# Token-major projections: four PSUM banks in turn instead of twelve matmuls to one

## The reference, cut to what matters

```python
proj = h @ w_in[l]                                    # first block: q, k, v, o, gates, z, u, qc
kv = mn @ w_kv                                        # memory keys and values (km, vm)
x = x + jnp.concatenate([y_a, y_b, y_c], axis=-1) @ w_out[l]
p = jnp.einsum('btd,de->bte', h, w_in[l]) + b_in[l]   # second block: a_u, a_v, q, k, v, r, ...
h = layer_norm(DEEPNORM_ALPHA * h + m @ w_out[l], ln1_g[l], ln1_b[l])
f = jnp.square(jax.nn.relu(h @ w_ff1[l])) @ w_ff2[l]
h = layer_norm(DEEPNORM_ALPHA * h + f, ln2_g[l], ln2_b[l])
```

## Time and profile before

| | |
|---|---|
| executions | 1139.32, 1141.18, 1141.46 us; median 1141.18 |
| span of the profiled execution | 1139.6 us (the profile gives no other time for it) |
| PE busy | 1114.3 us, 98% of the span, 5404 matmuls |
| PEld busy | 934.6 us, 82% |
| DVE, ACT, POOL busy | 601.2, 419.0, 85.9 us |
| mean DMA rate | 101 GB/s |
| mean granted TensorE clock | 0.989 |

### The profile page before, as it was taken

How to read it: one execution, slowest core, us unless ns; L and a number is a source line. 1 busy time by engine, 2 the same in 40 slices (tenths; PEclk the granted TensorE clock), 3 DMA queues, 4 the chain that set the end, 5 groups by cost and what they waited for, 6 DMA issues and landing times.

```text
span 1139.6 us, 13000 instructions
## 1 busy us (share of the span) xinstructions
PE 1114.3 (98%) x5404; PEld 934.6 (82%) x5404; DVE 601.2 (53%) x668; ACT 419.0 (37%) x446; POOL 85.9 (8%) x95
## 2 busy tenths in 40 slices
PE   8999999999999999999699999999999999999996
PEld 8788888887888888888588888888888888888885
DVE  5553357546544565558465654766332334435446
ACT  7444442543343422343333633332232223332330
POOL 3000000000022000006200000121000000000002
PEclk8999999999999999999799999999999999999999
DMA  8523421223324422231222222361423323323221
GB/s 280 180 77 111 147 75 40 82 74 111 111 75 159 126 104 74 80 124 38 74 74 74 77 72 74 108 224 59 126 78 106 109 75 111 98 86 111 78 70 74
DMA packets 82737, 114.79 MB, mean 101 GB/s; under 512 B 4316, under 2 KB 57948, under 8 KB 82560
## 3 DMA queue, kind: packets, MB, share of 16 engines
q1 hardware_dynamic: 79648, 103.19, 27.7%
q0 software_dynamic: 2752, 10.76, 2.7%
q10 hardware_dynamic: 288, 0.13, 0.0%
HBM read 109.87 MB, written 4.20 MB: 100 GB/s over the span
## 4 chain that ended last, share of the span: by engine, by line
PE 89%; DVE 5%; POOL 2%; issue 2%; ACT 1%; DMA 0%; DVEq 0%; POOLq 0%; SPq 0%; ACTq 0%
PE bank L369 27%; PE bank L371 27%; PE bank L370 27%; PE bank L477 2%; PE bank L671 1%; DVE w_lo L1162 1%; POOL rstd_tmp L1781 1%; DVE residual L1599 1%; PE bank L597 1%; PE bank L578 1%; DVE bn L1466 1%; PE bank L727 1%; PE bank L630 1%; PE bank L615 1%; DVE v_hat L1473 1%
## 5 line engine op out<-in xcount | busy, mean ns | idle before, releaser
L1162 DVE TENSOR_TENSOR w_lo<-w_raw,w_hi 128x2048 fp32r<-128x2048 f32 (+1 forms) x92 | 209.7, 2281 | 281.3 <-ACT w_hi L871 279.1
L369 PE MATMUL bank<-act_t_hi,w_hi 128*128 128x512 f32 (+1 forms) x832 | 321.4, 386 | 11.2 <-ACT u_gelu L1048 10.7
L371 PE MATMUL bank<-act_t_hi,w_lo 128*128 128x512 f32 (+1 forms) x832 | 318.2, 382 | 0.0
L370 PE MATMUL bank<-act_t_lo,w_hi 128*128 128x512 f32 (+1 forms) x832 | 317.9, 382 | 0.0
L871 ACT ACTIVATE w_hi<-w_raw 128x2048 fp32r<-128x2048 f32 (+1 forms) x91 | 172.0, 1892 | 204.1 <-PE bank L371 191.6
L369 PEld LDWEIGHTS bank<-act_t_hi,w_hi 128*128 128x128 f32 x832 | 157.2, 189 | 41.8 <-issue 11.7
L371 PEld LDWEIGHTS bank<-act_t_hi,w_lo 128*128 128x128 f32 x832 | 157.0, 189 | 30.5
L370 PEld LDWEIGHTS bank<-act_t_lo,w_hi 128*128 128x128 f32 x832 | 157.3, 189 | 29.9 <-issue 0.2
L369 PE MATMUL bank<-w_hi,x_hi 128*128 128x512 f32 x416 | 162.2, 390 | 0.0
L371 PE MATMUL bank<-w_hi,x_lo 128*128 128x512 f32 x416 | 161.9, 389 | 0.0
L370 PE MATMUL bank<-w_lo,x_hi 128*128 128x512 f32 x416 | 161.8, 389 | 0.0
(11 more groups left out here) (262 smaller groups left out, 1077.6 us busy)
## 6 DMA issues: line engine op xcount, KB each, us to landing
w_raw<-in_w_in SPq DMA_DIRECT2D x46, 1024.0 KB, 5.1
w_raw<-in_w_ff SPq DMA_DIRECT2D x32, 1024.0 KB, 5.2
w_raw<-in_w_out SPq DMA_DIRECT2D x10, 1024.0 KB, 5.2
w_raw<-in_w_mem_kv SPq DMA_DIRECT2D x3, 1024.0 KB, 6.6
residual<-in_x SPq DMA_DIRECT2D x4, 512.0 KB, 9.6
x_spill<-residual POOLq DMA_DIRECT2D x1, 2048.0 KB, 7.1
residual<-x_spill POOLq DMA_DIRECT2D x1, 2048.0 KB, 9.7
out<-residual SPq DMA_DIRECT2D x3, 512.0 KB, 2.6
```

The source lines that it names most:

```text
L369: pe.matmul(dst, lh, rh, start=start, stop=False)
L370: pe.matmul(dst, lh, rl, start=False, stop=False)
L371: return pe.matmul(dst, ll, rh, start=False, stop=stop)
L1162: return dve.tensor_tensor(dst, src, hi.bitcast(f32), ALU.subtract)
```

## The change

In every weight block of a token-major accumulation but the last, the loops are turned around. A new helper goes, for each kk, through the tiles with high times high, then through the tiles with high times low, then with low times high, so that successive matmuls go to banks 2, 3, 4, 5 in turn. The last block keeps the old order, and so does `tm_pair`. In the first block (g = 0) all banks are taken before the first matmul. The number of matmuls and their operands are the same.

```diff
+            def three_rotating(tiles, lh, ll, rh, rl, start):
+
+                for j in range(tiles):
+                    pe.matmul(bank[2 + j][:, :], lh[:, tile_of(j)], rh, start=start, stop=False)
+                for j in range(tiles):
+                    pe.matmul(bank[2 + j][:, :], lh[:, tile_of(j)], rl, start=False, stop=False)
+                for j in range(tiles):
+                    last = pe.matmul(bank[2 + j][:, :], ll[:, tile_of(j)], rh, start=False, stop=False)
+                return last
...
 (tm_block)
-                for j in range(tiles):
+                if g < groups - 1:
+                    if g == 0:
+                        for j in range(tiles):
+                            take(2 + j, ("tm", n, j))
+                    for kk in range(4):
+                        xh, xl = lhs(kk)
+                        last = three_rotating(tiles, xh, xl, wh[:, kk, :], wlo[:, kk, :], g == 0 and kk == 0)
+                        if between and kk == 1:
+                            between()
+                for j in range(tiles if g == groups - 1 else 0):
                     key = ("tm", n - g, j)
-                    if g == 0:
-                        take(2 + j, key)
                     for kk in range(4):
                         xh, xl = lhs(kk)
                         last = three(bank[2 + j][:, :], xh[:, tile_of(j)], xl[:, tile_of(j)], wh[:, kk, :], wlo[:, kk, :],
-                                     g == 0 and kk == 0, g == groups - 1 and kk == 3)
-                    if g == groups - 1:
-                        give(last, key)
+                                     False, kk == 3)
+                    give(last, key)
...
 (group, the matmuls of ff2)
+                    if g < 7:
+                        if g == 0:
+                            for j in range(TT):
+                                take(2 + j, ("tm", n0, j))
+                        for kk in range(4):
+                            h, l = lhs(kk)
+                            last = three_rotating(TT, h, l, wh[:, kk, :], wlo[:, kk, :], g == 0 and kk == 0)
+                        last.then_inc(w_used, 1)
+                        return
                     for j in range(TT):
-                        key = ("tm", n0, j)
-                        if g == 0:
-                            take(2 + j, key)
                         for kk in range(4):
                             h, l = lhs(kk)
                             last = three(bank[2 + j][:, :], h[:, tile_of(j)], l[:, tile_of(j)], wh[:, kk, :], wlo[:, kk, :],
-                                         g == 0 and kk == 0, g == 7 and kk == 3)
-                        if g == 7:
-                            give(last, key)
-                    if g < 7:
-                        last.then_inc(w_used, 1)
+                                         False, kk == 3)
+                        give(last, ("tm", n0, j))
```

## The result

The changed kernel takes 1144.40 us (median of nine runs, 1143.01 to 1145.77); the kernel before, run beside it, 1140.15 us (nine runs, 1138.92 to 1141.63). The ratio is 1.0036, 95% interval [1.0026, 1.0046]: 4.2 us slower. The forecast was 4.1 us slower, 1145.3 us; that figure started from 1141.18 us for the kernel before, the median of the first three of these nine runs.

A forecast was written before the change was run, and what follows sets the result against it. PE, busy 98% of the span, was taken as the bound: number of matmuls times distance between starts, plus gaps. Rotation 0 and waits 1.11 + 1.18 + 1.24 + 0.58 = 4.11 us on 1141.2 gave 1145.3 us, range 1142.3 to 1147.8.

The forecast's parts named there:

- The distance does not change: In the 1128 rotated matmuls the distance between starts stays 226.7 ns, so the rotation itself costs 0.
- the bound before: Limit drawn from rows on the rotation's effect: 13.3 ns a matmul, 15.0 us saved or lost over 1128 matmuls.
- The four waits: At four first blocks PE waits for all banks before the first matmul: 4.11 us in all.
- the slow restart: After a wait the second matmul follows after 0.32 us, not 0.227: 0.09 us more where the block did not already start so.
- second half of `ff2`: PE waits for DVE's reader of bank 5 where this half starts: 1.02 + 0.09 = 1.11 us.
- second columns of `w_out`: PE waits for bank 5's reader where these columns start: 1.09 + 0.09 = 1.18 us.
- `v2`: At its start PE waits for DVE's cumulative sums over the gate logits in banks 2 to 5: 1.24 us.
- `o`: Behind `v`, PE waits for ACT to free bank 5: 0.58 us, the slow second matmul being there already.
- Nothing takes it back: The 10.7 us wait moves along, as the ACT and DVE work behind it waited for the last bank of `a_v`.
- A quicker stream: Rival: each rotated matmul saves 13.3 ns paid for repeating a bank, 15.0 us won, 4.1 lost: 1130.3 us; chance 0.06.
- Hidden waits: Rival: the waits at the takes are there but mostly hidden: 1141.2 to 1143.3 us; chance 0.10.
- Lost clock: Rival: the four gaps or the rotation drop the granted clock to 1.2 GHz, 9.8 us more: 1155 us; chance 0.04.

The follow-up runs named there:

- The late reader: Changed kernel plus two DVE subtractions between the last matmul to bank 5 in the first half of `ff2` and that bank's reader: 1146.90 us, ratio 1.0055.
- the two rotation runs: Changed kernel with rotation only in blocks neither first nor last: ratio 1.0000; with first blocks rotated over banks 2 and 3, then 4 and 5: 0.9997.
- takes alone: Kernel before, old matmul order, but all banks taken before the first matmul of each accumulation's first block: 1144.61 us, ratio 1.0033.
- the two late readers: Two DVE subtractions added ahead of bank 5's reader in the first half of `ff2`: in the changed kernel ratio 1.0055, in the kernel before 1.0000.
- the first four experiments: takes alone 1.0033; changed kernel with rotation only in blocks neither first nor last, 1.0000; rotation by pairs 0.9997; lazy takes 1.0015; kernel before beside them 1140.53 us.
- rotation by pairs: Changed kernel, but first blocks rotate over banks 2 and 3, then 4 and 5, each pair taken when needed: 1140.29 us, ratio 0.9997.
- lazy takes: Changed kernel, but each bank is taken just ahead of its own first matmul: 1142.42 us, ratio 1.0015.
- other banks: Changed kernel, but the second half of `ff2` accumulates in banks 6, 7, 0 and 1: 1143.65 us, ratio 1.0024.
- the second changed profile: Profile of the changed kernel run again, unmodified, on the same chip as other banks: 1145.67 us, ratio 1.0044.

## Why the prediction was right

*The distance does not change.* Forecast 0 for 1128 matmuls; measured 226.68 ns in the half of `ff2` that is mostly rotated, against 226.66, and a ratio of 0.9997 for all of them rotated with the takes out of the way. The interval of that run allows 1.4 us saved to 0.7 us lost, 1.2 ns saved to 0.6 lost a matmul; the bound before was 13.3. The comparison of a stretch with 12 matmuls to a bank to one with 24 had said so in advance. The Trainium skill (TensorE: Matmul & The Clock Gate, section "Wait — 56ns, not 53.3ns?") has 215.7 ns from start to start of back-to-back matmuls of 512 columns at full clock; the trace has 226.7 in every order tried, so the repeated bank is not what makes up the difference.

*The four waits.* The mechanism was the forecast one, and no term is off by more than 0.02 us, so the sum owes nothing to errors that cancel. Each term against its measure, the wait and the slow restart together:

| place | forecast | measured | from |
|---|---|---|---|
| second half of `ff2` | 1.11 | 1.12 | 1046.31 - 1045.06 - 0.227, + 0.10 (1.17 for four instead of 1.07) |
| second columns of `w_out` | 1.18 | 1.19 | 315.69 - 314.36 - 0.227, + 0.09 |
| `v2` | 1.24 | 1.26 | 402.45 - 401.05 - 0.227, + 0.09 |
| `o` | 0.58 | 0.60 | 110.05 - 86.44 against 110.65 - 87.64 |
| sum | 4.11 | 4.17 | 4.22 by the stretch from `v` to the end |

*What the working had wrong.* Two things, and neither is a term of the sum. The waits of 10.7 and 1.0 us are not "nearly all" of PE's list before: it adds up to 16.3 us, and 4.0 of the rest are the waits for `mem`, `ones` and `mem_t_lo` in the first 90 us, a stretch that the four takes don't touch. And three waits of 1.0 to 1.2 us were to show in the list, which has 0.87, 0.94 and 1.01: the list counts from the end of the last matmul's row, 0.39 us after its start, and the sum from where the next matmul would have started, 0.227 us after it. The median itself came out 0.9 us under the forecast 1145.3, since the kernel before ran at 1140.15 us and not at 1141.18.

*Nothing takes it back.* The 10.7 us wait for `u_gelu` is 10.7 us in both profiles: what PE waits for there moved along with PE. The late reader shows the same for one longer wait: 2.27 us more wait, 2.25 us more in `ff2`.

*The rivals.* A quicker stream is excluded by the two rotation runs. Hidden waits are excluded by takes alone and by the two late readers. Lost clock did not come: the mean granted clock is 0.990 after and 0.989 before, and in both profiles it is 1.00 from `v` to 537 us, with three of the four waits, and from 563 us to the end of `ff2`, with the fourth. The Trainium skill (same page, section "A second HAM failure mode: psum-queue depth-cycling") ties going round the banks to small idle bits and a swinging clock. Here 1128 matmuls went round the banks (four, two in `vm`), at the old distance and with no clock lost, and the gaps that the takes made cost their own length and 0.1 us of restart. In this kernel, going round the banks did not by itself bring what that section describes.

## What to carry to other kernels

When matmuls in a stream stand at the same distance whether the bank changes or not, the order of banks is free, and only what it does to the moment at which each bank must be free counts. An accumulation that reuses the banks of the one before it needs time between the last matmul to a bank and the first new one. At `ff2` that is 1.25 us from start to start: 0.42 until the reader starts (0.39 of it the matmul's own row), 0.69 for the reader, 0.14 until PE goes on. Tile by tile that time is filled by the other tiles' matmuls; rotated over all the banks there are none to fill it. If a rotation is wanted for another reason, rotating over half of the banks in the first block or taking other banks removed the wait here.

## What the runs showed of the hardware that was not expected

Runs of one kernel spread by 2 to 3 us, and the spread goes with the clock. Of the 28 executions of the kernel before beside the first four experiments, the six at a mean granted clock of 0.992 took 1139.55 to 1139.76 us, the eleven at 0.989 took 1141.21 to 1141.87. The profiles show two places where it can arise. One is the first 30 us: with a granted clock of 0.87 to 0.90 over 12 to 30 us `v` starts at 87.64 to 87.82 us (seven profiles), with 1.00 at 85.96 to 86.44 (three). The other is the stretch behind the single long wait. After the 10.7 us wait the matmuls stand 0.427 us apart until the clock comes back. In the profile of before that is so for eleven distances, ten of them between the two rows; in rotation by pairs it is so for five, though the wait was the same:

```profile
553.10 0.77 PE L369 MATMUL bank<-act_t_hi,w_hi 128*128 128x512 f32 x1 [10.72 <-ACT u_gelu L1075]
...
555.37 0.63 PE L371 MATMUL bank<-act_t_hi,w_lo 128*128 128x512 f32 x1
555.79 0.46 PE L369 MATMUL bank<-act_t_hi,w_hi 128*128 128x512 f32 x1
556.09 0.39 PE L370 MATMUL bank<-act_t_lo,w_hi 128*128 128x512 f32 x1
```

Six distances fewer at 0.2 us each are 1.2 us, which is the -1.26 of that run in the table. Late reader in the changed kernel has five as well (5.28 + 1.2 = 6.5, expected 6.6), lazy takes nine (0.98 + 0.4 = 1.4, expected 1.5), takes alone, other banks and the first changed profile twelve, the second changed profile eleven. Up to `ff2` the late reader's program is the changed one, so five, eleven and twelve come from one and the same order of instructions. The span of one profile can thus be off by over 1 us here, while the same wait agrees within 0.02 us from one kernel's profile to the next (0.87 us at `ff2` in the changed kernel and in takes alone).

The other thing is that in the profiled executions waits of PE of up to 3.1 us cost no clock, while the one of 10.7 us did (0.72 over 538 to 562 us in both kernels). For the 3.1 us this is one profile, and the execution of 1149.38 us leaves it open whether it always holds.
